# A row per mLSTM head, spread over 128 partitions: eight-row matmuls replaced by a DMA with stride zero

## The reference, cut to what matters

```
b = jnp.cumsum(fc, axis=-1)                      # fc = log_sigmoid(forget gate)
d = jnp.where(causal, b[..., :, None] - b[..., None, :] + ic[..., None, :], NEG_INF_2)
inter = b + m_st[..., None]
m_i = jnp.maximum(jnp.max(d, axis=-1), inter)
s = jnp.einsum('bhid,bhjd->bhij', qc, kc) * jnp.exp(d - m_i[..., None])
num = jnp.einsum('bhij,bhje->bhie', s, vc) + ...
den = jnp.sum(s, axis=-1) + ...
h = num / jnp.maximum(jnp.abs(den), jnp.exp(-m_i))[..., None]
```

## Time and profile before

| what | value |
|---|---|
| three timed runs | 2190.05, 2192.61, 2192.63 us; median 2192.61 |
| the profiled execution | 2193.17 us, of which the span is 2191.4 us |
| granted TensorE clock | 0.999 of full speed |
| busy: PE / PEld / DVE / ACT / POOL | 99% / 82% / 61% / 49% / 3% |
| DMA | 418.84 MB, mean 191 GB/s |
| weight loads from SP | 512 KB each, 3.5 to 4.7 us from issue to landing |

### The profile page before, as it was taken

The page is one execution under the profiler, slowest core; times in us unless marked ns, Lnnn a source line. Parts: engine busy times, 40 slices in busy tenths (PEclk is TensorE's granted clock), DMA queues, the critical chain, the costliest instruction groups (busy, mean ns, idle before and its releaser), DMA issues.

```text
span 2191.4 us, 27409 instructions
## 1 busy us (share of the span) xinstructions
PE 2166.9 (99%) x9986; PEld 1789.9 (82%) x9986; DVE 1346.2 (61%) x1795; ACT 1078.5 (49%) x1500; POOL 59.2 (3%) x70
## 2 busy tenths in 40 slices
PE   8999999999999999999999999999999999999999
PEld 6888887888888888888878888888888888788887
DVE  5898857654555555555677545556445766666764
ACT  6444565654443444444465444454444555554442
POOL 0000100000000000000000000000000010000000
PEclk9999999999999999999999999999999999999999
DMA  8565446566666566666565665555666564555875
GB/s 313 182 191 162 147 145 217 183 183 193 210 184 197 186 192 189 187 191 190 175 195 185 201 192 172 172 169 178 203 201 201 173 193 143 165 181 171 326 241 164
DMA packets 117238, 418.84 MB, mean 191 GB/s; under 512 B 13169, under 2 KB 13425, under 8 KB 116849
## 3 DMA queue, kind: packets, MB, share of 16 engines
q1 hardware_dynamic: 115216, 411.04, 59.5%
q0 software_dynamic: 1744, 5.77, 0.9%
q10 hardware_dynamic: 144, 0.28, 0.0%
HBM read 406.55 MB, written 10.49 MB: 190 GB/s over the span
## 4 chain that ended last, share of the span: by engine, by line
PE 81%; DVE 2%; issue 0%; ACT 0%; POOL 0%; ACTq 0%; DVEq 0%
PE g L576 25%; PE g L578 25%; PE g L577 25%; PE s L555 2%; PE s L797 0%; PE s L796 0%; DVE wlo L1427 0%; DVE ta_lo L1602 0%; PE s L729 0%; PE s L728 0%; PE s L804 0%; DVE arena L1595 0%; PE s L671 0%; ACT whi L896 0%; PE s L738 0%
## 5 line engine op out<-in xcount | busy, mean ns | idle before, releaser
L1427 DVE TENSOR_TENSOR wlo<-raw,whi 128x1024 fp32r<-128x1024 f32 x734 | 893.9, 1222 | 610.8 <-ACT whi L896 609.3
L896 ACT ACTIVATE whi<-raw 128x1024 fp32r<-128x1024 f32 x734 | 772.7, 1057 | 666.1 <-PE g L578 660.8
L576 PE MATMUL g<-whi,ta_hi 128*128 128x512 f32 x1920 | 765.0, 398 | 11.6 <-DVE wlo L1427 9.3
L578 PE MATMUL g<-whi,ta_lo 128*128 128x512 f32 x1920 | 750.0, 391 | 0.0
L577 PE MATMUL g<-wlo,ta_hi 128*128 128x512 f32 x1920 | 748.5, 390 | 0.0
L576 PEld LDWEIGHTS g<-whi,ta_hi 128*128 128x128 f32 x1920 | 361.3, 188 | 85.1 <-issue 13.3
L578 PEld LDWEIGHTS g<-whi,ta_lo 128*128 128x128 f32 x1920 | 361.0, 188 | 77.5
L577 PEld LDWEIGHTS g<-wlo,ta_hi 128*128 128x128 f32 x1920 | 361.7, 188 | 71.9
L576 PE MATMUL g<-whi,tb_hi 128*128 128x512 f32 x1008 | 399.4, 396 | 0.2 <-ACT arena L1078 0.2
L578 PE MATMUL g<-whi,tb_lo 128*128 128x512 f32 x1008 | 393.5, 390 | 0.0
L577 PE MATMUL g<-wlo,tb_hi 128*128 128x512 f32 x1008 | 392.8, 390 | 0.0
(11 more groups left out here) (218 smaller groups left out, 923.9 us busy)
## 6 DMA issues: line engine op xcount, KB each, us to landing
raw<-in_w_in SPq DMA_DIRECT2D x320, 512.0 KB, 4.1
raw<-in_w_up SPq DMA_DIRECT2D x128, 512.0 KB, 3.5
raw<-in_w_down SPq DMA_DIRECT2D x128, 512.0 KB, 3.6
raw<-in_w_out SPq DMA_DIRECT2D x64, 512.0 KB, 4.1
raw<-in_w_a SPq DMA_DIRECT2D x32, 512.0 KB, 4.1
raw<-in_w_b SPq DMA_DIRECT2D x32, 512.0 KB, 4.7
raw<-in_w_ukv SPq DMA_DIRECT2D x16, 512.0 KB, 4.0
raw<-in_w_uq SPq DMA_DIRECT2D x12, 512.0 KB, 3.6
```

The lines of the kernel that those rows point to most:

```text
L576: e.matmul(o, xh, wh, start=first, stop=False)
L578: ins = e.matmul(o, xl, wh, start=False, stop=last)
L896: e.activation(whi[u % RING][:, 0:n], raw[u % RAW][:, 0:n], ACT.Copy).then_inc(s_hi, 1)
L1427: e.tensor_tensor(l, r, h.bitcast(F32), ALU.subtract).then_inc(s_lo, 1)
```

## The change

PE's eight-row matmul is gone. SP writes M of all heads to DRAM (8 KB), and later reads it back in two DMAs of four heads each, whose source has stride zero in its first dimension: every partition gets the same 4 KB. The two targets (`F2`) are 512 KB each. DVE's line 1825 and ACT's line 1215 read `F2` in place of PSUM. DVE's wait for the scores (`ml_s`) moves from part "a" to part "s".

```
+        F2 = [ar(12320, 1024).rearrange("p (h n) -> p h n", h=4), ar(17196, 1024).rearrange("p (h n) -> p h n", h=4)]
...
 # PE, ml_side
                         if part == "s":
-                            f1, f2 = bank(0, (ml_st, h + 1)), bank(1, (ml_e, h + 1))
+                            f1 = bank(0, (ml_st, h + 1))
                             w, k = QK2[:, h, :], QK2[:, 8 + h, :]
                             q.wait_ge(row_d, 1)
                             q.wait_ge(qk2_r, 8)
-                            e.matmul(f2[:, 0:256], CST[0:8, h:h + 1].to_broadcast([8, P]), ROWS[6], start=True, stop=True)
                             e.matmul(f1[:, 0:256], k[:, 0:P], w, start=True, stop=True)
...
 # ACT, ml_side
+                            q.wait_ge(d_f2, 32)
-                            e.activation(E3[:, 1], sps[1][:, P:256], ACT.Exp, bias=uN[:, h:h + 1], scale=-1.0)
+                            e.activation(E3[:, 1], F2[h // 4][:, h % 4, P:256], ACT.Exp, bias=uN[:, h:h + 1], scale=-1.0)
...
 # DVE, ml_side
                         if part == "a":
                             E3 = ML_E[i].rearrange("p (c n) -> p c n", c=3)
                             q.wait_ge(d_cst, 16)
-                            q.wait_ge(ml_s, h + 1)
+                            q.wait_ge(d_f2, 32)
                             if h >= 2:
                                 q.wait_ge(ml_st, h - 1)
-                            e.tensor_tensor(E3[:, 0:3:2, :], mk, sps[1][:, 0:256].rearrange("p (c n) -> p c n", c=2),
+                            e.tensor_tensor(E3[:, 0:3:2, :], mk, F2[h // 4][:, h % 4, :].rearrange("p (c n) -> p c n", c=2),
                                             ALU.subtract).then_inc(ml_a, 1)
                         elif part == "s":
+                            q.wait_ge(ml_s, h + 1)
                             q.wait_ge(ml_e, h + 1)
...
 # SP, a new side
+            def row_side():
+                yield E("small") + 13
+                q.wait_ge(row_e, 1)
+                e.dma_start(d["rows"], ROWS[6]).then_inc(d_rows, 16)
+                yield E("qk23") + 10
+                q.wait_ge(d_rows, 16)
+                q.wait_ge(qk2_r, 8)
+                for m in range(2):
+                    e.dma_start(F2[m], d["rows"][4 * m:4 * m + 4].unsqueeze(0).to_broadcast([P, 4, 256])).then_inc(d_f2, 16)
```

More of the change, by code:

```diff
@@ L330, in two_blocks @@
         d_xt = [sem(f"d_xt{i}") for i in range(8)]
-        d_cst, d_vec, d_pos, d_xr, d_pg, d_pg2, d_x2s = (sem(n) for n in (
-            "d_cst", "d_vec", "d_pos", "d_xr", "d_pg", "d_pg2", "d_x2s"))
+        d_cst, d_vec, d_pos, d_xr, d_pg, d_pg2, d_x2s, d_rows, d_f2 = (sem(n) for n in (
+            "d_cst", "d_vec", "d_pos", "d_xr", "d_pg", "d_pg2", "d_x2s", "d_rows", "d_f2"))
         d_bias = [sem(f"d_bias{i}") for i in range(4)]
@@ L2238, in sync @@
                 load(p)
-            sides = [Side(g) for g in (x_side(), gain_side(), x2_side(), spill_side(), y_side(), out_side(), store_side())]
+            sides = [Side(g) for g in (x_side(), gain_side(), row_side(), x2_side(), spill_side(), y_side(), out_side(), store_side())]
             for slot, units in slots_and_splits():
@@ L2369 @@
         aps[name] = nc.dram_tensor(f"keep_{name}", (4, 128, 1024), F32).ap()
+    aps["rows"] = nc.dram_tensor("keep_rows", (8, 256), F32).ap()
     out = nc.dram_tensor("out_0", (256, 2048), F32, kind="ExternalOutput").ap()
```

## The result

The changed kernel takes 2186.55 us (median of 11 runs, 2183.40 to 2187.34), the kernel before 2192.60 (11 runs beside them, 2190.05 to 2193.07). The ratio is 0.9973, 95% interval 0.9965 to 0.9980: 6.05 us faster. The forecast was 2186.1, 6.5 us less.

What follows compares the result with a forecast made beforehand. PE was taken to bound the kernel at the heads: eight heads by 0.81 us gave 6.5 less, other terms 0. Against the 2192.61 median that made 2186.1 us, 0.30% faster, range 2183.0 to 2189.8.

Steps and rivals of the forecast that it cites:

- PE sets the time at the heads: Eight heads, 1325 to 1500 us: PE waits for no other engine, so time taken out of PE shortens the kernel.
- The size: 1.62 - 0.81 per head, 6.5 in all: PE at each head, dense matmul to dense matmul: 1.62 us falls to 0.81; eight heads give 6.5 us.
- all three gaps: Ahead of lines 728, 729 and 730 at each head: 0.09, 0.19 and 0.10 us, all expected to go.
- the neighbour at part "o": Lines 737 and 738, same head: 0.23 us after the dense matmul, then 0.43, taken as the shape after the change.
- Part of the gap stays: Rival at the heads: line 729 inherits 728's waits and its load might stop; 5.0 us less, 2187.6, chance 0.16.
- only the stream goes: Rival at the heads: the 0.38 us of gaps show up elsewhere; 3.4 us less, 2189.2, chance 0.08.
- DVE and ACT: New source SBUF: ACT 24 ns more per head, DVE unchanged; 0.44 us of cover less the 24 ns at part "o".
- the moved wait, taken as a gain alone: DVE's wait for scores at odd heads, 1.5 us over four: moving it takes that off, so they get cover.
- SP and the DMAs at 0: SP and DMA queues: waits cost nothing, write nothing to 4.1 us hidden, read pair 6.0 us covered; term 0.
- The cover of 12.9 us: Weight loads behind the pair: 4.4 us until ACT's split is delayed plus 8.5 behind it, until PE stops.
- the full rate of the DMA engines: From 199 GB/s at 0.65 busy around 1205 to 1245 us: 306 GB/s, at least 3.4 us for the pair.
- The rival of slow reads: Stride-zero reads delay weight loads; at 24 us PE stops 11.1, 2197.2; chance 0.08, shared with some other late load.

Runs made afterwards that it cites:

- 128-row variant: Kernel before, each head's eight-row matmul made 128 rows high, added rows multiplied by zero; 2190.82 us against 2192.52, ratio 0.9992.
- 32 rows: Kernel before, each head's eight-row matmul made 32 rows high; read from the profile only: 1.62 us dense to dense, 165.75 us for the heads' stretch.
- pairs: Kernel before, eight-row matmuls of both heads of a pair issued back to back at the even head; 2192.26 us against 2192.52, ratio 1.0002.
- the run with the DMAs alone: Kernel before plus the write and two reads, DVE waiting for them, nothing reading them, eight-row matmuls kept; median 2190.50 us, ratio 0.9995.
- The run with the doubled subtraction: Changed kernel, DVE's subtraction (mask minus the row) done twice at each head; median 2187.71 us, ratio to before 0.9972.
- one wave more: Changed kernel with 2.0 MB more stride-zero reads behind the pair, 3.0 MB in all; 2187.34 us in one run.

## Why the prediction was right, by its steps

**PE sets the time at the heads.** Right. The stretch of the heads gave back all that was taken out of PE, 6.56 us by the traces.

**The size: 1.62 - 0.81 per head, 6.5 in all.** Right in the sum, 0.82 measured per head, and in its parts. The stream of 0.43 us is what the second eight-row matmul costs behind the first, and is left over when the stops are taken away (1.23 - 0.80). The stops of 0.38 are what the 128-row variant saves (3.05 / 8). The step that could have failed was the claim that all three gaps would go with line 728, and the neighbour at part "o" was the right row for it. The row count as their cause was read from one kind of row then; the variants with 128 and 32 rows and with pairs show it.

**The rivals with a smaller gain.** Part of the gap stays (5.0) and only the stream goes (3.4): both fell, on the distances of 0.23 and 0.43. The Trainium skill ("TensorE: Matmul & The Clock Gate", "LDWEIGHTS (loading the stationary operand)" and "Why this matters for your kernels") says that the rows do not matter to a single matmul. For the matmul's own stream the runs agree: 0.43 us for an eight-row one behind another, and 0.43 for one of 128 rows. For its place in a sequence they do not: 1.62 us from dense to dense with 8 and with 32 rows, 1.23 with 128. The measurement decides.

**DVE and ACT.** The mechanism was right, the size slightly off: 0.32 us of cover instead of 0.42, of which 10 ns are ACT's 402 ns instead of 392. Most of the rest stands ahead of DVE's product: from the start of ACT's last exponential to it 0.49 us (1330.73 to 1331.22), before 0.42 (1333.87 to 1334.29). In the run with the DMAs alone, where the wait for the scores is still at the subtraction, it is 0.42 as before. So the moved wait, taken as a gain alone, is the likely cost; it was not tried by itself. The run with the doubled subtraction shows that PE would have paid soon after.

**SP and the DMAs at 0.** Right: no wait of PE after, none with the DMAs alone. 6.0 us were taken for the pair and some 7.4 measured from its first issue. The cover of 12.9 us was measured as 12.8, with 8.3 instead of 8.5 for the part behind ACT's split. One bound was wrong without harm: the full rate of the DMA engines, worked out as 306 GB/s. With one wave more, they moved 415 GB/s from 1220 to 1225 us at a share of 1.01, so by an estimate from this rate the least time for the pair is 2.5 us (1.05 MB) and not 3.4. The rival of slow reads has fallen for this size: even 3.0 MB did not reach PE.

**The median.** 2186.1 forecast, 2186.55 measured. That these lie so close is in part luck, for a median of such runs depends on how many of them lost time to the clock: five of the 11 after have a mean clock of 0.998. Among runs of the same clock the medians before (27 runs, taken with the experiments) and after differ by 6.2 to 6.7 us. In the range, 2189.2 and half a microsecond are 2189.7, not 2189.8.

## What to carry to other kernels

Where PE is the bound, read the distance between starts around a small matmul, and what PEld does there, rather than the matmul's own duration: here an operand of 8 rows cost 0.82 us, of which the matmul was 0.43. If the small matmul can't be moved off PE, fill its rows up to 128 with zeros and its columns up to 128 with anything whose output is not read, or set several of one shape behind each other. And before a transfer is put on the queue of the weight loads, add up how late a load may be before PE stops; here it was 12.8 us, and the pair of 512 KB, there after 7.4, stayed inside it.

## What the runs showed of the hardware that was not expected

- A narrow stationary operand also stops the load: 8 and 64 columns 0.35 us behind dense 128x128 loads, 128 columns none. Operands of 72 columns behind ones of 128 did not stop it.
- The same short pause of PE is followed by a lower clock in some executions and not in others. Behind 2.0 us of standing still near 263 us the granted clock of 6 us is 0.72 in eight of the twelve traces (dense matmuls start 0.43 us apart instead of 0.23: the level of 1.2 GHz) and 1.00 in four; behind 2.5 us near 1866 us it is 0.72 in four. Each fall costs 1.5 to 1.6 us. In those eight traces PE starts again at the first place at 262.9 to 263.8 us, in the other four at 262.2 to 262.6; whether the one makes the other is not shown. For a saving below 3 us the trace is the better witness: the pairing variant saved 1.60 us in its stretch, and its median moved by 0.3.
- Behind a stop of 9.86 us the clock was 0.67 from 1240 to 1250 us, so the stop cost more than its length: 12.8 us in the trace, 12.1 between the medians.
- With one wave of reads more, the DMA engines moved 395 GB/s from 1215 to 1220 us and 415 from 1220 to 1225, at shares of 0.99 and 1.01. The rate worked out from a busy share of 0.65 was 306.
